# x loaded and turned by column halves, three low halves made by adding DMAs, and one split moved

## The reference

```
x = x + 0.5 * swiglu(rms(x))            # 1024 -> 2 x 2816 -> 1024, first feed-forward
h = rms(x); z = h @ w_in + b_in         # windowed attention and a gated spatial mix
x = x + concat(A, B) @ w_out + b_out
x = x + 0.5 * swiglu(rms(x))            # second feed-forward, other weights
x = x + sigmoid(rms(x) @ w_ple_gate) * (p @ w_ple_proj)   # p: 520 rows of width 256
y = rms(x) * g_final
```

## Time and profile before

| | |
|---|---|
| median of 3 runs | 987.37 us |
| the profiled execution | 986.51 us |
| its span in the trace | 984.8 us |
| TensorE busy | 98% of the span |
| VectorE / ScalarE / GpSimd busy | 68% / 47% / 26% |

### The profile page before, as it was taken

One profiled execution on the slowest core, in us unless ns is written; L12 is line 12 of the kernel. 1 busy time (PEld: TensorE's weight loads), 2 busy tenths in 40 slices (PEclk: granted clock), 3 DMA queues, 4 the chain that ended last, 5 costly groups with the idle time before them and its releaser, 6 DMA issues.

```text
span 984.8 us, 19296 instructions
## 1 busy us (share of the span) xinstructions
PE 963.6 (98%) x7949; PEld 947.1 (96%) x7949; DVE 672.4 (68%) x1063; ACT 458.7 (47%) x750; POOL 260.5 (26%) x150
## 2 busy tenths in 40 slices
PE   6999999999999999999999999999999999999997
PEld 4999999999999999999899999999999999999997
DVE  5899658856768654457775399857766758855576
ACT  6645425533435443566444455424543443545243
POOL 2302202211111226332318411301221211114521
PEclk9999999999999999999999999999999999999999
DMA  7962433252243336321114693253324325235202
GB/s 216 163 127 70 124 105 99 76 145 72 75 128 99 97 85 184 102 65 44 44 55 129 128 172 97 61 145 97 96 80 116 97 60 144 65 98 161 87 22 88
DMA packets 191603, 101.38 MB, mean 103 GB/s; under 512 B 12955, under 2 KB 189429, under 8 KB 191501
## 3 DMA queue, kind: packets, MB, share of 16 engines
q1 hardware_dynamic: 175904, 90.23, 32.2%
q0 software_dynamic: 11440, 5.77, 4.7%
q10 hardware_dynamic: 4172, 4.15, 1.4%
HBM read 97.59 MB, written 3.59 MB: 103 GB/s over the span
## 4 chain that ended last, share of the span: by engine, by line
PE 91%; DVE 5%; ACT 1%; DMA 1%; issue 1%; SPq 0%; DVEq 0%; ACTq 0%
PE ps L1723 49%; PE ps L1803 36%; PE ps L2141 2%; PE ps L1759 1%; DMA x_rows<-in_x_prompt_dram 1%; PE ps L2015 1%; PE ps L2044 1%; DVE w_lo L1327 0%; PE ps L1754 0%; DVE w_lo L1419 0%; PE ps L1748 0%; DVE xb_lo L1216 0%; DVE tt L1437 0%; DVE mix_lo L1550 0%; PE ps L2165 0%
## 5 line engine op out<-in xcount | busy, mean ns | idle before, releaser
L1803 PE MATMUL ps<-xo_hi,w_hi 128*128 128x260 f32 x1008 | 284.2, 282 | 0.7 <-DVE ab L1350 0.7
L1803 PE MATMUL ps<-xo_lo,w_hi 128*128 128x260 f32 x1008 | 284.7, 282 | 0.0
L1803 PE MATMUL ps<-xo_hi,w_lo 128*128 128x260 f32 x1008 | 284.4, 282 | 0.0
L1723 PE MATMUL ps<-h_hi,w_hi 128*128 128x260 f32 x960 | 195.8, 285 | 0.7 <-issue 0.6
L1723 PE MATMUL ps<-h_hi,w_lo 128*128 128x260 f32 x960 | 193.4, 283 | 0.0
L1723 PE MATMUL ps<-h_lo,w_hi 128*128 128x260 f32 x960 | 193.4, 283 | 0.0
L1803 PEld LDWEIGHTS ps<-xo_hi,w_hi 128*128 128x128 f32 x1008 | 189.6, 188 | 0.9 <-issue 0.9
L1803 PEld LDWEIGHTS ps<-xo_hi,w_lo 128*128 128x128 f32 x1008 | 189.8, 188 | 0.0
L1803 PEld LDWEIGHTS ps<-xo_lo,w_hi 128*128 128x128 f32 x1008 | 189.7, 188 | 0.0
L1723 PEld LDWEIGHTS ps<-h_hi,w_hi 128*128 128x128 f32 x960 | 148.1, 189 | 1.7 <-issue 1.2
L1723 PEld LDWEIGHTS ps<-h_lo,w_hi 128*128 128x128 f32 x960 | 148.8, 189 | 0.0
(11 more groups left out here) (276 smaller groups left out, 1476.5 us busy)
## 6 DMA issues: line engine op xcount, KB each, us to landing
w_raw<-in_w_ffn_dram SPq DMA_DIRECT2D x88, 256.0 KB, 3.0
w_a<-in_w_ffn_dram SPq DMA_DIRECT2D x36, 512.0 KB, 4.8
w_raw<-in_w_ffn_dram SPq DMA_DIRECT2D x48, 384.0 KB, 3.2
w_raw<-in_w_ffn_dram SPq DMA_DIRECT2D x16, 512.0 KB, 7.0
w_lo<-in_w_ffn_dram POOLq DMA_DIRECT2D x11, 512.0 KB, 8.4
w_raw<-in_w_in_dram SPq DMA_DIRECT2D x10, 512.0 KB, 4.0
w_raw<-in_w_ple_gate_dram SPq DMA_DIRECT2D x8, 512.0 KB, 3.6
x_rows<-in_x_prompt_dram SPq DMA_DIRECT2D x4, 512.0 KB, 5.7
```

The lines of the kernel that those rows point to most:

```text
L1723: ins = pe.matmul(ps[:, bank + step * h, 0:HALF], w[:, c, w0:w0 + P], m_[:, sk, h * HALF:(h + 1) * HALF], start=(first and n == 0), stop=( ...
L1803: ins = pe.matmul(ps[:, b, 0:Q], w[:, c, k * P:(k + 1) * P], m_[:, op, k, :], start=(first and k == 0 and n == 0), stop=(k == 3 and n == 2 ...
```

## The change

- **Head.** x is loaded in eight pieces, the left column halves (tiles 0 to 3) of the four blocks first; weight tile "up" 0 is loaded between the left and the right halves. The samples are turned once, into one bank. The turns go by block inside a half, so that TensorE waits only for the piece that it turns. VectorE copies tiles 0, 2, 3, 5 and ScalarE 1, 4, 6, 7, without the samples. The low halves of "up" 0 to 3 are made on VectorE (`first_lo`) between other steps; "up" 2 and 3 are no longer `summed`, and GpSimd makes none of the first ones. The row squares are cut in two halves. The ten small vectors are loaded by SyncE behind "up" 1. `first_stat_out` (the spread of `rstd`) moves from step 5 of "up" 1 to step 3 of "up" 2.
- **Operands.** B11 lies in `bbuf`, the second quarter in the bytes of `sq` and `ssq`, B21 and B22 in the bytes of `xo_hi` of T3 and T4 (`b2x`). ScalarE makes the high half of B21, B22 and B11 and writes minus it into `xo_lo`; GpSimd issues three DMAs that add the fp32 operand onto it, behind that of "up" 7. The high half of T3 (T4) waits for the added B21 (B22). VectorE makes four low halves instead of seven.
- **p.** `p_hi` and `p_lo` are made inside the feed-forward, behind `x_add` of tile 6.

```diff
-B11, B21, B22, U1, T3, U2, T4 = range(7)
-XO_ORDER = (B11, U1, U2, B21, B22, T3, T4)
+B11, B21, B22, U1, U2, T3, T4 = range(7)
+X_BY_DVE = (0, 2, 3, 5)
+X_BY_ACT = (1, 4, 6, 7)
+XO_HI = (B21, B22, B11, U1, U2, T3, T4)
+XO_ADDED = (B21, B22, B11)
+XO_LO = (U1, U2, T3, T4)
...
-        2: [("w", "up", 6), ("swi_b", 0), ("xn", 4), ("xn", 5), ("xn", 6), ("xn", 7), ("xsum", 0), ("xsum", 1)],
-        3: [("w", "up", 7), ("swi_a", 1), ("xsum", 2), ("xsum", 3), ("xo_hi", 0), ("xo_hi", 1), ("xo_hi", 2)],
-        4: [("swi_b", 1), ("xo_lo", 0), ("xo_lo", 1), ("xo_hi", 3), ("xo_hi", 4)],
-        5: [("swi_a", 2), ("xo_hi", 5), ("xo_hi", 6), ("xo_lo", 2), ("xo_lo", 3), ("xo_lo", 4), ("xo_lo", 5)],
+        2: [("w", "up", 6), ("swi_b", 0), ("xn", 4), ("xn", 5), ("xn", 6), ("xn", 7), ("xo_hi", B21), ("xo_neg", B21),
+            ("xo_hi", B22), ("xo_neg", B22), ("xo_hi", B11), ("xo_neg", B11), ("xsum", 0), ("xsum", 1)],
+        3: [("w", "up", 7), ("swi_a", 1), ("xsum", 2), ("xsum", 3), ("xo_hi", U1), ("xo_hi", U2),
+            ("xo_add", B21), ("xo_add", B22), ("xo_add", B11)],
+        4: [("swi_b", 1), ("xo_lo", U1), ("xo_lo", U2)],
+        5: [("swi_a", 2), ("xo_hi", T3), ("xo_lo", T3)],
         6: [("w_sum13", 0), ("w_hi_a", 0), ("swi_b", 2), ("w_sum24", 0), ("w_hi_13", 0), ("w_lo_a", 0),
             ("w_hi_24", 0)],
...
-        7: [("w_lo_13", 0), ("w_hi_22", 0), ("swi_a", 3), ("w_lo_24", 0), ("w_lo_22", 0), ("xo_lo", 6)],
+        7: [("w_lo_13", 0), ("w_hi_22", 0), ("swi_a", 3), ("w_lo_24", 0), ("w_lo_22", 0), ("xo_hi", T4), ("xo_lo", T4)],
...
                     if c == 3 and m in (4, 5):
                         steps.append(("p_turn", m - 4))
+                    elif c == 3 and m == 6:
+                        steps.append(("p_split",))
...
+        b12 = sqs[:].rearrange("p a (h t) -> p (a h) t", t=Q)
...
+                skip(under, 5 * 4 * Q * 4, "skip_b2x")
+                b2x = sb("b2x", [P, 2, 4, Q], scope=under)
...
-        summed = [("up", 0, n) for n in range(2, N_STD)] + [("up", 1, n) for n in range(3, N_STD)]
+        summed = [("up", 0, n) for n in range(4, N_STD)] + [("up", 1, n) for n in range(3, N_STD)]
...
+            for h, landed in enumerate((x_in, x_in_right)):
+                for b in range(NB):
+                    part = slice(h * 512, (h + 1) * 512)
+                    sp_.dma_start(x_rows[:, b, part], a["x_prompt"][0, b * P:(b + 1) * P, part]).then_inc(landed[b], 16)
+                if h == 0:
+                    load(("up", 0, 0), w_dram["w1_ffn1"][:, :, 0:P])
+            load(("up", 0, 1), w_dram["w3_ffn1"][:, :, 0:P])
...
+                        op, = arg
+                        if op in XO_ADDED:
                             act.wait_ge(xn_made, 8 * s + 8)
+                        elif op in (T3, T4):
+                            act.wait_ge(xo_summed, 4 * s + 4)
+                            act.wait_ge(xo_added[(T3, T4).index(op)], 16 * (s + 1))
                         else:
                             act.wait_ge(xo_summed, 4 * s + 1 + (U1, T3, U2, T4).index(op))
-                        nc.scalar.activation(xo_at(xo_hi, op), xo_at(xo_raw, op),
-                                             ACT.Copy).then_inc(xo_hi_ready, 1)
+                        nc.scalar.activation(xo_at(xo_hi, op), xo_source(op), ACT.Copy).then_inc(xo_hi_ready, 1)
+                    elif kind == "xo_neg":
+                        op, = arg
+                        act.wait_ge(xo_hi_ready, 7 * s + XO_HI.index(op) + 1)
+                        nc.scalar.activation(xo_at(xo_lo, op), xo_at(xo_hi, op).bitcast(F32), ACT.Copy,
+                                             scale=-1.0).then_inc(xo_negated, 1)
...
+            x_copy(1)
+            first_hi(0)
+            split_hi(("up", 0, 0))
+            for m in range(1, KD):
+                if m > 1 and m in X_BY_ACT:
+                    x_copy(m)
+                first_hi(m)
+            split_hi(("up", 0, 1))
+            split_hi(("up", 0, 2))
...
+                    elif kind == "xo_add":
+                        op, = arg
+                        i = XO_ADDED.index(op)
+                        pool.wait_ge(xo_negated, 3 * s + i + 1)
+                        pool.dma_start(xo_at(xo_lo, op), xo_source(op), accum_op=ALU.add).then_inc(xo_added[i], 16)
...
-            for n in range(3):
-                split_lo(("up", 0, n))
...
+            for m in X_BY_DVE[0:3]:
+                x_copy(m)
+            dve.wait_ge(x_by_dve, 4)
+            x_lo(0, 0)
+            first_lo(0)
+            for m in range(1, 4):
+                x_lo(0, m)
+            x_copy(5)
+            dve.wait_ge(x_by_dve, 5)
+            for m in range(4, KD):
+                x_lo(0, m)
+            first_lo(1)
             for b in range(2, NB):
-                dve.wait_ge(x_in[b], 16)
-                link(nc.vector.tensor_tensor_reduce(out=sq_rows[:, 0, :], in0=x_rows[:, b, :], in1=x_rows[:, b, :],
-                                                    scale=1.0, scalar=0.0, op0=ALU.mult, op1=ALU.add,
-                                                    accum_out=rs_t[:, b:b + 1]))
-            dve.wait_ge(cols_ready, 1)
-            for m in range(0, KD, 2):
-                dve.wait_ge(x_turned, m + 1)
-                take_turned(x[:, m, :], 1 + m % 3).then_inc(x_even, 1)
-                if m:
-                    x_lo(0, m - 1)
-                x_lo(0, m)
-            x_lo(0, KD - 1)
-            stat_diag(0)
+                dve.wait_ge(x_in_right[b], 16)
+                row_square(b, slice(512, D), rs_t)
+            dve.wait_ge(row_sums, 4)
+            link(nc.vector.tensor_tensor(rs_t[:, 0:NB], rs_t[:, 0:NB], rs[:, 0:NB], ALU.add))
+            first_lo(2)
             dve.wait_ge(cols_turned, 2)
             nc.vector.tensor_copy(cols[:, KD:N_COLS], ps[:, 7, KD:N_COLS]).then_inc(cols_ready, 1)
+            stat_diag(0)
+            first_lo(3)
...
-                                between = [(6, lambda: stat_out(2))] if s else [(1, vectors), (5, first_stat_out)]
+                                between = [(6, lambda: stat_out(2))] if s else [(1, vectors)]
+                            elif not s:
+                                between = [(3, first_stat_out)]
...
+            for h, landed in enumerate((x_in, x_in_right)):
+                for b in range(NB):
+                    pe.wait_ge(landed[b], 16)
+                    for m in range(4 * h, 4 * h + 4):
+                        if h and b == 0:
+                            if m - 4 in X_BY_ACT:
+                                pe.wait_ge(x_by_act, X_BY_ACT.index(m - 4) + 1)
+                            else:
+                                pe.wait_ge(x_by_dve, X_BY_DVE.index(m - 4) + 2)
+                        ins = turn(ps[:, 2 + m % 4, b * P:(b + 1) * P], x_rows[:, b, m * P:(m + 1) * P])
+                        if b == NB - 1:
+                            ins.then_inc(x_turned, 1)
...
```

More of the change, by code:

```diff
@@ L459, in hybrid_decoder_layer @@
         x_in = [sem(f"x_in{i}") for i in range(NB + 1)]
+        x_in_right = [sem(f"x_in_right{i}") for i in range(NB)]
+        samples_turned, up_lo = sem("samples_turned"), sem("up_lo")
         p_in, ps_in = sem("p_in"), sem("ps_in")
@@ L554, in flat, with xo_source @@
             return ap.rearrange("p a t -> p (a t)")
+        def xo_source(op):
+            if op == B11:
+                return flat(bbuf[:])
+            if op in (B21, B22):
+                return flat(b2x[:, op - B21, :, :])
+            return xo_at(xo_raw, op)
         def banks(first, step):
@@ L821, in ffn_stage @@
                         x_hi(2 * s + 1, arg[1])
+                    elif kind == "p_split" and s:
+                        act.wait_ge(p_ready, KP)
+                        nc.scalar.activation(p_hi[:], p_t[:], ACT.Copy).then_inc(pple_hi, 1)
             act.dma_start(rows[0:KD, :], a["g_ffn1"][0].rearrange("(k p) -> k p", p=P)).then_inc(gain_in, 16)
             act.dma_start(xs_rows[0:TS, :], a["x_sample"].rearrange("b t d -> (b t) d")).then_inc(x_in[NB], 16)
[L825 to L836, removed]
             act.wait_ge(consts_ready, 2)
@@ L1004, in _ @@
             ffn_stage(1)
-            act.wait_ge(p_ready, KP)
-            nc.scalar.activation(p_hi[:], p_t[:], ACT.Copy).then_inc(pple_hi, 1)
             for key in last_keys(1)[3:6]:
@@ L1398, in _ @@
[L1398 to L1406 removed]
+                    elif kind == "p_split" and s:
+                        dve.wait_ge(pple_hi, 1)
+                        nc.vector.tensor_tensor(p_lo[:], p_t[:], p_hi[:].bitcast(F32), ALU.subtract).then_inc(pple_lo, 1)
@@ new lines, in x_copy, with first_lo, row_square @@
+            def x_copy(m):
+                dve.wait_ge(x_turned, m + 1)
+                nc.vector.tensor_copy(x[:, m, 0:TP], ps[:, 2 + m % 4, :]).then_inc(x_by_dve, 1)
+            def first_lo(n):
+                key = first_up[n]
+                dve.wait_ge(w_hi_ready, index[key] + 1)
```

(17 more changed lines are left out.)

115 lines of the change are left out of this document (63 added, 52 removed).

## The result

The changed kernel takes 997.49 us (median of 4 runs, 997.1 to 998.68) beside 986.75 for the kernel before (4 runs, 985.55 to 987.81): ratio 1.0113, 95% interval 1.0101 to 1.0125. It is slower, as forecast, by 10.7 us where 7.3 were forecast. The profiled execution took 998.68, with a span of 996.9 us beside 984.8; it is the longest of the four, so its span differs by 12.1 us where the medians differ by 10.7.

What follows compares the result with a forecast made beforehand. TensorE, busy 98%, was taken to bound the kernel, with VectorE as full among the first three units. Head -0.4, second feed-forward +8.8, end -1.1 gave +7.3: 994.2 us, own range 990.5 to 997, 8 in 10 985.5 to 998.5.

Steps and rivals of the forecast that it cites:

- rival 3: Both feed-forwards: adding DMAs share engines with weight loads, land 2 us later and stall TensorE; about +12.5, 999; chance 13%.
- B21's transfer: Second feed-forward: the adding DMA onto B21 lands at 596.5, between 592.4 and 598, and T3's pass waits for it.
- Rival 1: B21's adding DMA lands early because the queue overlaps transfers; -1.0 in all, 985.5 to 986.5; chance 15%.
- rival 2: Units of both feed-forwards: VectorE works off its lateness; between -5.4 and -0.4, about 983; chance 12%.
- Rival 4: Head: right pieces of x land late, "up" 0 starts at 15, first feed-forward loses 2 more: 996; chance 5%.
- The low clock behind TensorE's idle time: Second feed-forward: TensorE running slower after 5 idle us costs nothing, as it has 3.9 us over VectorE to lose.
- The 7.3 us of the head shrink to 0.4: First feed-forward: of the head's 7.3 us, 0.4 remain after the wait for B21; bounds 4.4 gained to 1.5 lost.
- TensorE turns four pieces in 1.09, so its turns end at 12.5: Head: the turns of x end last, at 12.5, so "up" 0 starts at 12.6 instead of 19.94.
- VectorE's last combination at 99.73 stays there: First feed-forward: VectorE's last combination keeps its time of 99.73, and TensorE gains only 0.5.
- The end: End of the kernel: TensorE's wait of 1.07 for `p_lo` goes; -1.1, range 0 to -1.1.

## Why the prediction was right, and where its sizes were off

**The number** has luck in it. 997.49 lies inside the range for 8 in 10 (985.5 to 998.5), but above the forecast's own range (990.5 to 997), and the upper bound that holds it was taken from rival 3, which did not happen. From span to span the forecast +7.3 became +12.1: 3.1 more in the first feed-forward, 0.5 more in the second, 1.3 in the mixer and 0.2 behind the units, which had no term, and 0.3 less at the end.

**The mechanism** was right step by step in the second feed-forward and at the end. These are times of after less the 4.1 us of its later row scale: "up" 7's DMA issued at 587.1 (forecast 587.4), T3 released at 596.3 (596.5), `w_sum13` at 598.6 (598.75). VectorE was 8.7 late there (8.8), and TensorE 9.3. VectorE was full, as the forecast asked: 31.25 us busy of the 32.38 from 613.20 to 645.58. B21's transfer, the one unknown price, had been bounded between 592.4 and 598 and taken at 596.5: its DMA landed 8.3 behind its issue for a forecast 7.6, and was issued 0.9 sooner. Rival 1 (it lands early) fell by 4 us; rival 2 (VectorE works its lateness off) fell by the table above; rival 3's total was near, but not its mechanism, since "up" 7 stalled nothing. Rival 4 came in part: "up" 0 started at 13.86, halfway to its 15; what made it late is the first step below. Two sums of the rivals are off by a little: rival 1's terms give -0.9, not -1.0, and rival 3's 12.7, not 12.5.

The low clock behind TensorE's idle time had been taken at nothing. The windows behind the wait of 4.80 us show it at 1.2 GHz, and VectorE full:

```profile
604.00:608.00 4.00, 0.08 (x1) 0.00 (x0) 3.65 (x6) 1.51 (x2) 0.00 (x0) 0.99 0.61 151
608.00:612.00 4.00, 3.12 (x14) 3.12 (x15) 4.00 (x4) 2.44 (x4) 1.91 (x1) 0.50 0.00 0
612.00:616.00 4.00, 4.00 (x25) 4.00 (x24) 3.78 (x6) 3.81 (x6) 0.00 (x0) 0.65 0.71 197
```

At that place it cost at most the 0.6 between 8.7 and 9.3, since VectorE sets the time.

**The term that failed** is "The 7.3 us of the head shrink to 0.4": the first feed-forward came 2.7 later instead of 0.4 earlier. Three sizes make it up.
- The step "TensorE turns four pieces in 1.09, so its turns end at 12.5". The rows behind it gave the price of four turns and the landing of the last piece. But 16 right turns stood in a row from 10.54, 0.21 us each, behind the first right piece and behind copies that began at 9.05 instead of 7.0, because 16 left turns came first too. "up" 0 started at 13.86 instead of 12.6, the row scale came 1.75 us earlier (VectorE's first product with it at 31.27 for 33.02) and not 3.0, and B21's first pass at 40.05 instead of 38.8.
- B21 landed 9.6 behind the issue of "up" 7's DMA, not 9.1. With the head, `w_sum13` came at 60.61 instead of 58.75, so 2.85 later than before, and VectorE's former wait of 0.84 for TensorE could take up only that much: the next unit's came at 71.39 for 69.29, 2.1 late.
- "VectorE's last combination at 99.73 stays there" was wrong by 3.0. Those 2.1 us stayed to the end, and 0.9 to 1.1 came on top where VectorE works beside GpSimd. Two instructions of VectorE and the `h_lo` of GpSimd beside them, before and after:

```profile
94.52 1.23 DVE L1359 TENSOR_TENSOR ab<-ab,bb 128x1040 f32<-128x1040 f32 x1
95.67 3.46 DVE L1327 TENSOR_TENSOR w_lo<-w_raw,w_hi 128x1024 fp32r<-128x1024 f32 x1
94.58 3.47 POOL L1101 TENSOR_TENSOR h_lo<-ab,h_hi 128x1040 fp32r<-128x1040 f32 x1 [8.26 <-ACT h_hi L818]
```

```profile
96.41 3.48 DVE L1409 TENSOR_TENSOR ab<-ab,bb 128x1040 f32<-128x1040 f32 x1
99.81 2.31 DVE L1377 TENSOR_TENSOR w_lo<-w_raw,w_hi 128x1024 fp32r<-128x1024 f32 x1
96.16 2.63 POOL L1154 TENSOR_TENSOR h_lo<-ab,h_hi 128x1040 fp32r<-128x1040 f32 x1 [9.37 <-ACT h_hi L868]
```

VectorE's two take 4.69 together before and 5.79 after, at the same work. Who begins first differs. Before, VectorE was 0.06 us ahead: its first instruction took 1.23, and `h_lo` 3.47. After, GpSimd was 0.25 ahead: `h_lo` took 2.63, and VectorE's instruction 3.48. Each stretched instruction of VectorE ends 1.1 us behind one of GpSimd (99.13 and 98.05 before; 99.89 and 98.79, then 102.12 and 101.05, the end of GpSimd's next `w_lo`, after), as if it had waited for it. That this order makes the 1.1 us is read from these rows, not tried.

**The end** gave 1.4 for a forecast 1.1, with no wait for `p_lo` and none for `xb_lo` in its place.

**The page weighed against the rows.** The shortest landing of an operand was 8.3 us. An estimate from the Trainium skill, DMA: Bandwidth & Descriptors, section Anatomy of one DMA, was 3.2 us; here the measurement decides, and it lies beyond even the 6.6 of an adding DMA by itself. In the changed kernel "up" 7 still landed 6.6 behind its issue in the second feed-forward, and the three behind it 2.5 to 3.1 us apart, so at least they queued; no run has an operand's DMA by itself.

## What to carry to other kernels

Work taken from a full engine is worth what it is worth at the place where that engine is full: here VectorE was spared 3.5 us per feed-forward ahead of the units, spent them idle behind ScalarE and a DMA, and came late into the 31 us in which it has no slack. Before an operation is handed to a DMA, ask who else reads its target in program order; moving back one pass, which waited for B21 and stood behind a displaced tanh, recovered 11 us with the transfer as slow as before. The best version here keeps the head and the moved split, and leaves the operands alone: 982.2 us, and 983.0 when it was run again.

## What the runs showed of the hardware that was not expected

- A DMA that adds 520 KB of SBUF onto SBUF lands 8.0 to 13.2 us after issue when three go out in a burst behind one from memory, 8.7 to 11.1 when they go out 2.07 us apart. They land 2.5 to 3.1 us apart in both cases; between 598 and 603 us, where they do so in the changed kernel, the core's DMA moved 204 to 220 GB/s. In a burst an issue lasts 1.6 to 2.3 us on GpSimd, though the next begins 0.6 us behind it; apart from each other they last 0.85 to 1.1.
- Of two instructions with large fp32 operands, VectorE's 128x1040 and GpSimd's 128x1040, begun 0.06 to 0.25 us apart, the later one took 0.8 to 2.3 us longer: VectorE 3.48 for 1.23, GpSimd 3.47 for 2.63.
- One kernel in two executions had its fall of the granted clock 26 us apart in the mixer, at the same total (spans 996.9 and 996.5); the later fall was half as long. The wait of TensorE for `mix_lo` went with it: 2.46 us where the clock had stayed up, 0.99 where it had fallen ahead of the wait. A single profile's wait can be such a trade, so it is read together with the PEclk of the stretch ahead of it.
